# Hybrid two-block model on one core: ten more weight pieces multiplied as split halves instead of plain fp32, with VectorE's and ScalarE's order changed

## What is computed

```
proj  = h @ w_in                          # GLU, z, x, B, C, dt and gate columns
conv_out = conformer_conv_branch(u_glu, ...)   # GLU, 31-tap depthwise conv, LayerNorm, SiLU, @ pw_w
# ssd_branch, 8 groups of 256 inner channels:
xbc = silu(causal_depthwise_conv(xbc, conv_w, conv_b))
y   = ssd_chunked(x, dt, a, B, C, d_skip)
y   = y * silu(z)
yg  = y.reshape(.., 8 groups, 256)
yg  = yg * rsqrt(mean(yg * yg) + eps)     # per group
out = (yg * norm_g) @ out_w
mixed = (g_conv * conv_out + g_ssm * ssm_out) @ w_out
```

## Time and profile before

| | us |
|---|---|
| median of 3 executions | 910.43 |
| lowest, highest | 910.02, 910.46 |
| the profiled execution, device time | 910.08 |
| its span from the first to the last instruction | 908.0 |
| TensorE busy | 899.3 (99%) |
| VectorE busy | 736.6 (81%) |
| ScalarE busy | 580.8 (64%) |
| GpSimd busy | 38.0 (4%) |

### The profile page before, as it was taken

One profiled execution on the slowest core, in us unless ns is written; L12 is line 12 of the kernel. 1 busy time (PEld: TensorE's weight loads), 2 busy tenths in 40 slices (PEclk: granted clock), 3 DMA queues, 4 the chain that ended last, 5 costly groups with the idle time before them and its releaser, 6 DMA issues.

```text
span 908.0 us, 18312 instructions
## 1 busy us (share of the span) xinstructions
PE 899.3 (99%) x6623; PEld 847.7 (93%) x6623; DVE 736.6 (81%) x1361; ACT 580.8 (64%) x998; POOL 38.0 (4%) x50
## 2 busy tenths in 40 slices
PE   9999999999999999999999999999999999999997
PEld 7999999999999999998888888999999999999886
DVE  5999898888989988689888646889979988888533
ACT  5649878797877575566666535679656755666332
POOL 1000111111110000000000000100000000000000
PEclk9999999999999999999999999999999999999999
DMA  9577588877875647456555555445447455555601
GB/s 335 181 267 231 143 199 236 248 219 218 241 203 192 209 166 247 145 161 236 196 186 185 193 187 170 147 171 189 143 134 257 158 192 185 182 179 175 228 1 47
DMA packets 48510, 172.04 MB, mean 189 GB/s; under 512 B 5668, under 2 KB 6344, under 8 KB 48328
## 3 DMA queue, kind: packets, MB, share of 16 engines
q1 hardware_dynamic: 43488, 154.74, 51.2%
q0 software_dynamic: 2880, 10.49, 6.1%
q10 hardware_dynamic: 2088, 6.08, 1.8%
HBM read 159.72 MB, written 1.09 MB: 177 GB/s over the span
## 4 chain that ended last, share of the span: by engine, by line
PE 66%; issue 24%; DVE 6%; ACT 2%; DMA 1%; POOL 1%; SPq 0%; POOLq 0%; ACTq 0%; DVEq 0%
PE A L472 10%; PE A L473 10%; PE A L474 10%; PE B L696 5%; PE A L504 4%; PE B L504 3%; PE B L472 2%; PE B L473 2%; PE B L474 2%; PE A L506 2%; DVE w_lo L1397 2%; PE B L506 2%; PE B L777 2%; PE A L777 1%; PE A L485 1%
## 5 line engine op out<-in xcount | busy, mean ns | idle before, releaser
L1397 DVE TENSOR_TENSOR w_lo<-raw,w_hi 128x1024 fp32r<-128x1024 f32 x249 | 301.8, 1220 | 72.7 <-ACT w_hi L930 72.1
L930 ACT ACTIVATE w_hi<-raw 128x1024 fp32r<-128x1024 f32 x249 | 259.4, 1051 | 74.6 <-PE A L778 20.9
L472 PE MATMUL A<-h,w_hi 128*128 128x256 f32 x952 | 274.5, 288 | 0.2 <-DVE sc L2017 0.2
L474 PE MATMUL A<-h,w_lo 128*128 128x256 f32 x952 | 269.2, 283 | 0.0
L473 PE MATMUL A<-h,w_hi 128*128 128x256 f32 x952 | 269.2, 283 | 0.0
L472 PEld LDWEIGHTS A<-h,w_hi 128*128 128x128 f32 x952 | 182.1, 191 | 3.3 <-issue 2.6
L473 PEld LDWEIGHTS A<-h,w_hi 128*128 128x128 f32 x952 | 182.3, 191 | 0.3
L474 PEld LDWEIGHTS A<-h,w_lo 128*128 128x128 f32 x952 | 182.2, 191 | 0.0
L472 PE MATMUL B<-h,w_hi 128*128 128x256 f32 x352 | 100.1, 284 | 0.0
L473 PE MATMUL B<-h,w_hi 128*128 128x256 f32 x352 | 99.6, 283 | 0.0
L474 PE MATMUL B<-h,w_lo 128*128 128x256 f32 x352 | 99.6, 283 | 0.0
(11 more groups left out here) (313 smaller groups left out, 1635.0 us busy)
## 6 DMA issues: line engine op xcount, KB each, us to landing
raw<-in_weights_dram SPq DMA_DIRECT2D x289, 512.0 KB, 4.3
w_lo<-raw POOLq DMA_DIRECT2D x20, 512.0 KB, 4.8
csrow<-cs_dram ACTq DMA_DIRECT2D x9, 512.0 KB, 4.9
x<-in_x_dram SPq DMA_DIRECT2D x4, 256.0 KB, 5.3
bd<-in_lru_w_dram ACTq DMA_DIRECT2D x1, 1024.0 KB, 5.7
out_dram<-m_wide SPq DMA_DIRECT2D x3, 256.0 KB, 2.1
raw<-in_weights_dram SPq DMA_DIRECT2D x2, 256.0 KB, 4.8
par<-in_params_dram SPq DMA_DIRECT2D x1, 379.0 KB, 6.3
```

What stands on the lines that cost most here:

```text
L472: mm(dst, wh, lo, start=first, stop=False, skip_group_check=free)
L474: return mm(dst, wl, hi, start=False, stop=last, skip_group_check=free)
L930: F(w_hi[:, s, :], raw[:, s, :], ACT.Copy).then_inc(hi_ready, 1)
L1397: V.tensor_tensor(w_lo[:, s, :], raw[:, s, :], w_hi[:, s, :].bitcast(F32), ALU.subtract).then_inc(lo_ready, 1)
```

## The change

- `NATIVE` shrinks from 21 pieces to 11: what stays plain are GLU pieces 0 to 3 and the first output piece of each of the seven turns. The second output piece of each turn (37, 45, ... 85), pieces 94 and 95 and GLU piece 9 become split, ten in all.
- Seven more low pieces: 9, 85, 86, 88, 91, 94, 95 (27 instead of 20). The second output pieces of the loop (37 to 77) are split by VectorE.
- The operand of a split output piece has to be in halves: ScalarE writes `yn_hi` (`y_high`), VectorE `yn_lo` (`y_low`), of half c=1 in turns 1 to 7 and of both halves for pieces 94 and 95.
- VectorE's `lo()` calls move: none is left between the first convolution inputs and `cbm` in turns 1 to 7, and those of the turn stand behind `dec`, `y_gated` and before `moment`.
- ScalarE's list in a loop turn gets the high half of the turn's second output piece at its head.

```
-GLU_NATIVE = (0, 1, 2, 3, 9)
-NATIVE = frozenset(GLU_NATIVE) | frozenset([LOOP0 + 8 * i + n for i in range(GROUPS - 1) for n in OUT_AT]) | frozenset(range(TAIL0, PW0))
+GLU_NATIVE = (0, 1, 2, 3)
+NATIVE = frozenset(GLU_NATIVE) | frozenset([LOOP0 + 8 * i + OUT_AT[0] for i in range(GROUPS - 1)])
+EARLY_LOW = [GLU0 + 9]
+LAST_LOW = [GATES0 + n for n in (6, 7, 9, 12)] + [TAIL0, TAIL0 + 1]
...
 out_piece(p, turn, g, c, between=None):
-                native_loaded(p, turn)
-                pe.wait_ge(scale_read, g + 2)
+                split = p not in NATIVE
+                if split:
+                    split_ready(p, turn)
+                    pe.wait_ge(yn_low, g + 1)
+                else:
+                    native_loaded(p, turn)
+                    pe.wait_ge(scale_read, g + 2)
                 for m in range(KD):
                     ...
+                    if split:
+                        ins = tile(p % RING, m, yn_hi[:, c, :], yn_lo[:, c, :], acc_out(m), False, False, True)
+                        continue
...
 ScalarE
+            def y_high(g, cs=(1,)):
+                act.wait_ge(scale_read, g + 2)
+                for c in cs:
+                    ins = F(yn_hi[:, c, :], yn[:, c, :], ACT.Copy)
+                ins.then_inc(yn_high, 1)
 (loop turn)
+                split(0)
                 split(1)
                 split(2)
                 silu_bc(g)
+                y_high(g - 1)
...
 VectorE
+            def y_low(g, cs=(1,)):
+                dve.wait_ge(yn_high, g + 1)
+                for c in cs:
+                    ins = V.tensor_tensor(yn_lo[:, c, :], yn[:, c, :], yn_hi[:, c, :].bitcast(F32), ALU.subtract)
+                ins.then_inc(yn_low, 1)
 (group_turn)
                 if first:
                     conv_inputs(g, (0, 1))
+                    conv_inputs(g, (2, 3))
+                else:
                     lo()
-                    conv_inputs(g, (2, 3))
-                lo()
...
                 decayed_scores(g)
                 lo()
+                if first:
+                    y_low(g - 1)
...
                 y_gated(g)
-                lo(1 if first else 2)
+                lo(2)
...
                 if looped:
-                    lo()
+                    lo(2)
                     y_mean(g)
```

More of the change, by code:

```diff
@@ L77 @@
 PIECES = DOWN2 + KF2
-GLU_NATIVE = (0, 1, 2, 3, 9)
-NATIVE = frozenset(GLU_NATIVE) | frozenset([LOOP0 + 8 * i + n for i in range(GROUPS - 1) for n in OUT_AT]) | frozenset(range(TAIL0, PW0))
+GLU_NATIVE = (0, 1, 2, 3)
+NATIVE = frozenset(GLU_NATIVE) | frozenset([LOOP0 + 8 * i + OUT_AT[0] for i in range(GROUPS - 1)])
 LOW_AT = (1, 4, 7)
-LOW = [LOOP0 + 8 * i + n for i in range(GROUPS - 1) for n in LOW_AT if LOOP0 + 8 * i + n < GATES0 + LEAD]
+EARLY_LOW = [GLU0 + 9]
+LAST_LOW = [GATES0 + n for n in (6, 7, 9, 12)] + [TAIL0, TAIL0 + 1]
+LOW = EARLY_LOW + [LOOP0 + 8 * i + n for i in range(GROUPS - 1) for n in LOW_AT
+                   if LOOP0 + 8 * i + n < GATES0 + LEAD] + LAST_LOW
 UP1_TURNS = 2 * KF // RING
@@ L131, in split_order @@
 def split_order(p, turn=0):
-    return sum(q not in NATIVE and q not in LOW for q in range(p)) + 1 + (6 - len(LOW_AT) if p < GATES0 else 8) * turn
+    return sum(q not in NATIVE and q not in LOW for q in range(p)) + 1 + (7 - len(LOW_AT) if p < GATES0 else 8) * turn
 def low_turn(p):
-    return (p - LOOP0) // RING + 1
+    return sum(q <= p and q % RING == p % RING for q in LOW)
 STAGED_FFN1 = KD
@@ L190, in hybrid_kernel @@
         scale = sb("scale", [P, TT])
+        s0 = ExitStack()
+        yn_hi = sb("yn_hi", [P, 2, T], F32R, s0)
+        yn_lo = sb("yn_lo", [P, 2, T], F32R, s0)
+        s0.close()
         stage = sb("stage", [P, 2, T])
@@ L334, in hybrid_kernel @@
         neg_ready = sem("neg_ready")
-        low_added = {n: sem(f"low_added{n}") for n in LOW_AT}
+        low_added = {n: sem(f"low_added{n}") for n in sorted(set(p % RING for p in LOW))}
         constants_written = sem("constants_written")
@@ L446, in add_raw @@
                 nc.gpsimd.dma_start(w_lo[:, p % RING, :], raw[:, p % RING, :],
-                                    accum_op=ALU.add).then_inc(low_added[(p - LOOP0) % RING], 16)
+                                    accum_op=ALU.add).then_inc(low_added[p % RING], 16)
+            for p in EARLY_LOW:
+                add_raw(p)
             add_raw(LOOP0 + 1)
@@ L456, in _ @@
                 rsqrt(i + 3)
-            for n in range(GROUPS + 1, 17):
+            for p in LAST_LOW[:4]:
+                add_raw(p)
+            rsqrt(GROUPS + 1)
+            for p in LAST_LOW[4:]:
+                add_raw(p)
+            for n in range(GROUPS + 2, 17):
                 rsqrt(n)
@@ L490, in chunk_piece @@
                 if p in LOW:
-                    pe.wait_ge(low_added[(p - LOOP0) % RING], 16 * low_turn(p) + 16 * turn)
+                    pe.wait_ge(low_added[p % RING], 16 * low_turn(p) + 16 * turn)
                 else:
@@ L688, in y_scale, with split_ready @@
                 spread_scale(g + 2)
-            def out_piece(p, turn, g, c, between=None):
-                native_loaded(p, turn)
-                pe.wait_ge(scale_read, g + 2)
+            def split_ready(p, turn):
+                if p in LOW:
+                    pe.wait_ge(low_added[p % RING], 16 * low_turn(p) + 16 * turn)
+                else:
+                    pe.wait_ge(lo_ready, split_order(p, turn))
+            def out_piece(p, turn, g, c, between=None):
+                split = p not in NATIVE
[5 more added lines that the diff above has]
+                    pe.wait_ge(scale_read, g + 2)
                 for m in range(KD):
@@ L1127, in _ @@
             g = GROUPS - 1
-            for n in range(3):
-                split_hi(GATES0 + n + LEAD)
+            split_hi(GATES0 + LEAD)
             silu_bc(g)
+            split_hi(GATES0 + 1 + LEAD)
+            y_high(g - 1)
+            split_hi(GATES0 + 2 + LEAD)
             def conv_operand(c):
@@ L1150, in _ @@
                     F(gates[:, 0:KD, :], gates[:, 0:KD, :], ACT.Sigmoid).then_inc(gates_ready, 1)
+                if n == 7:
+                    y_high(g, (0, 1))
                 if n == 10:
@@ L1711, in group_turn @@
                     y_mean(g)
-                    lo()
+                    lo(2 if first else 1)
                 if more:
```

5 lines of the change are left out of this document (4 added, 1 removed).

## The result

| | before | after |
|---|---|---|
| median of 5 executions each, same chip, us | 910.18 | 915.10 |
| lowest, highest | 909.78, 910.46 | 913.89, 915.53 |
| the profiled execution, us | 910.08 | 915.17 |
| its span, us | 908.0 | 912.7 |

The change makes the kernel slower: after to before is 1.0052, with a 95% interval of 1.0040 to 1.0064. I had forecast 910.7, no change; 915.1 lies above the range.

A forecast was written before the change was run, and what follows sets the result against it. TensorE, busy 99% of the span, was taken to bound the kernel. Terms -0.58 + 1.0 + 0.6 + 0.2 + 0.2 - 1.15 = +0.3 us on the median 910.43 gave 910.7, no measurable change; range 908.2 to 914.3.

The forecast's parts named there:

- What a split piece saves: TensorE's output pieces: a plain one takes 3.46 us, a split one 2.88, so 0.58 less each, 5.8 for ten.
- The rival by which the change isn't what it says: Split output pieces take as long as plain ones, their halves being moving operands of another tile: 912.4 us; chance 0.02.
- Turns 1 to 6: Loop turns: a later `moment` makes TensorE wait 0.75 us for the scale; turns 27.76 instead of 27.59, +1.0 for six.
- The power: GpSimd's power between `moment` and the scale: 0.98 us in loop turns beside taps, 1.59 in turn 7 beside a split.
- From the scale to the next `cbm` the turn is TensorE's own, 10.34: Rest of a loop turn on TensorE: 27.59 - 17.25 = 10.34 us, with no piece in it getting cheaper.
- ScalarE in the turns, +0.6 for late loads: Loop turns: exponentials end at +3.95, `dec` starts at +4.08, just fitting; +0.6 us for one turn whose loads land late.
- The rival that ScalarE becomes the bound: Exponentials come 0.6 us later than `dec` wants them in six turns: +3.6, 914.3 us, slower; chance 0.20.
- The rival that TensorE keeps all: VectorE comes earlier than counted and no turn waits: 6.3 us less, 904.2; chance 0.10.
- Turn 7: Turn after the loop: `dec` 1.0 late through ScalarE, `moment` at +16.3, scale 1.89 behind it: +0.2 us.
- LayerNorm sums: End of the kernel: two `yn_lo`, 0.70 us, stand ahead of VectorE's squares, against a margin of 0.63: +0.2.
- Pieces 94 and 95: Output pieces at the LayerNorm sums: they took 3.70 and 3.62 us and lose 0.58 each: -1.15.
- GLU piece 9: GLU stage: -0.58 us; ScalarE's 2.06 and one adding DMA costed at nothing, covered by the ring's lead of six pieces.

The follow-up runs named there:

- e10: Changed kernel with scale a piece later, splits after `moment`, ScalarE's high half and `yn_hi` behind exponentials, piece 9 plain, turn 7's exponentials earlier: 905.02 us.
- e4: Changed kernel with TensorE's six loop turns written out one after the other instead of its `Fori`: 912.3 us, ratio 1.0026 to the kernel before.
- e3: Changed kernel with the scale's transposes inside the loop turn's last input piece, ahead of its last two blocks: 916.58 us, ratio 1.0074 to the kernel before.
- e11: Changed kernel with ScalarE's high half of the turn's second output piece and `yn_hi` moved behind the exponentials: 914.24 us, ratio 1.0044 to the kernel before.
- e1: Changed kernel with VectorE's `lo(2)` call ahead of `moment` moved behind the taps that follow it, in loop turns: 911.63 us, ratio 1.0019.
- e7: Changed kernel with TensorE's scale one input piece later, behind the next turn's first piece: 911.51 us, ratio 1.0018 to the kernel before.
- e2: Changed kernel with `moment` directly ahead of the `lo(2)` call, so a split runs beside GpSimd's power: 912.3 us, ratio 1.0028 to the kernel before.

## Why the prediction was wrong, point by point

- **What a split piece saves: right.** Output pieces 94 and 95 took 6.00 together instead of 7.02, from the first start to the first matmul of piece 96 (327.72 to 333.72, before 322.31 to 329.33), 0.51 less for each, and e10's turn is 0.61 shorter. The rival by which the change isn't what it says falls.
- **Turns 1 to 6: the mechanism right, the size wrong: +0.82 a turn instead of +0.17.** `dec` came at +4.08 and `y` at +9.84, as worked out. Then three terms went off, and they add up (0.17 + 0.29 - 0.11 + 0.47 = 0.82):
  - *`moment` at +16.42, not +16.13.* I took six taps as 2.40 "from start to start", 2.46 less an overlap. The rows of before say otherwise: from the first tap to `moment` it was 213.41 - 210.81 = 2.60, and 2.59 it was after. Not 2.40: that is 0.19. Another 0.10 fell on the wait between `y` and its product.
  - *The power* took 0.88 and not 0.98. With rounding and the step to TensorE that is -0.11; the scale came at +17.60, not +17.42.
  - *"From the scale to the next `cbm` the turn is TensorE's own, 10.34": the step that failed.* It was 10.81. I carried a stretch over from a turn in which TensorE hadn't waited. 0.43 of the 0.47 is the loop's end behind a wait (0.57 instead of 0.14 to the next matmul); 0.04 I can't place. Over the six turns this stretch grew by 2.6 us, where I had nothing: 0.46 to 0.51 in each of turns 1 to 5, and 0.19 in turn 6, which isn't followed by another. That is more than half of the miss of 4.4. e4 takes it away alone, and e3 moves it as worked out.

  TensorE itself was at the scale as forecast: its last matmul ahead of it starts at 219.40 and one takes 0.12, which is +16.64 against +16.67. It waited 0.96 by this count (0.80 by the record, whose tail runs on), and not 0.75, since the scale came 0.18 later than forecast. Counted from `cbm`, TensorE took the scale 2.4 us later over the six turns (0.90 in turn 1, 0.09 to 0.35 in the others), where 1.6 was forecast with the 0.6 for ScalarE. That the mean growth of a turn, 0.83, is just that of turn 4 is chance.
- **ScalarE in the turns, +0.6 for late loads: wrong, it was 0.** No `dec` waited for ScalarE in turns 1 to 6. In turn 4 the exponentials ended at +3.54, 0.4 before the +3.95 that I counted. The rival that ScalarE becomes the bound named nearly the right time, 914.3, by the wrong mechanism, so that this is luck: e11 relieves ScalarE and the time stays. It was right on the room, though: as soon as a turn falls to 27.9 (e1, e7), its exponentials are what is late.
- **The rival that TensorE keeps all**: refuted as the change stands; e10 shows it for the loop turns, with three orders altered.
- **Turn 7: right.** `dec` at +5.32 (I had 1.0 late; 0.93 of waiting), `moment` at +16.31 (+16.3), the scale at +18.23 (+18.2), the power 1.61 beside a split. TensorE took the scale 0.26 later after `cbm` than before (+0.2).
- **LayerNorm sums: +0.2 forecast, it was 0.** TensorE took the squares at +39.53 instead of +39.29, so turn 7's delay is all there is. They came 0.09 ahead of TensorE, which hid the two `yn_lo` (the margin had been 0.63).
- **Pieces 94 and 95: -1.14 against -1.15**, of which pieces 96 and 97 took back 0.42. I hadn't asked what waits there next.
- **GLU piece 9: -0.58 forecast; +0.15 at the `cbm` of turn 1 of the profiled execution, with 0.87 of waiting.** In this execution the step that failed is "one adding DMA, cost nothing, covered by the ring's lead of six pieces". Its copies on ScalarE were in time (the last from 25.93 on); the DMA itself, 11.47 us long among the loads, was not. In the eight other profiles the lead covered it, and the saving doesn't stand out there either, so why it isn't seen stays open. The price that I gave for missing cover, about 2.06, was ScalarE's and named the wrong resource.
- In sum, measured against forecast: turns 4.96 - 1.6 = 3.4, up to turn 1 0.15 + 0.58 = 0.7, the end -0.44 + 0.75 = 0.3: 4.4 by the two profiled executions, which is 915.1 - 910.7. Only the first of the three is more than the scatter of single executions.

## What to carry to other kernels

When an edit makes an engine wait where it did not wait before, don't carry the rest of the cycle over from the old trace: ask what the sequencer did ahead of time until now, above all at the end of a loop body, and put such a wait where plain work follows it, if that doesn't bring the engine to the wait earlier (e3 lost by it, e7 didn't). Read the distance between two starts in a row from the rows themselves, to the next instruction and not to the end of the group. And where three engines form a ring, an edit that relieves one cycle shows the next one within tenths of a microsecond (scale, then exponentials, then both): all must be opened before the saving is seen.

## What the runs showed of the hardware

- A wait as the last work of a loop body on TensorE cost 0.38 to 0.43 us a turn besides the wait: 0.57 from the scale's transposes to the next matmul, against 0.19 with the loop written out (e4) or with blocks behind the wait (e3), and 0.14 where nothing was awaited (before, e10). It was 0.33 in the last turn, which leaves the loop. It came in full in e1 too, where the power ended just in time and no idle time showed. What part is the branch, what part the fetch of the next instructions or the loop's register instructions, these runs don't tell.
- An adding DMA of one piece took 11.5 us from issue to landing beside the weight loads of the GLU stage in the changed kernel's profile, and 10.2 to 10.6 us in eight others with the same stage; no row tells what held it up in the one.
- GpSimd's power on 128x2 took 0.87 to 0.99 beside taps of 0.4 us and 1.59 to 1.66 beside a split of 128x1024 (1.22), in turn 7 and, with e2's order, in the loop alike.
